# Reordering four places of a second transformer block (gates, delta-rule rounds, latent attention, merge) in a fused Trainium2 kernel

## The reference, cut to what matters

```python
# h: modulated, normalised tokens (1024 channels); ctx: the same of the context
q, k, v = split(silu(centred_conv(h @ w_qkv, width 5)))      # 8 heads of 128
q, k = l2norm(q), l2norm(k)
beta = sigmoid(h @ w_beta)                                   # 8 heads, 2 directions
g = -exp(a_log) * softplus(h @ w_decay + dt_bias)            # log decays
# gated delta rule, both directions, S is 128 x 128 for each head:
#   S_t = exp(g_t) S_{t-1} (I - beta_t k_t k_t^T) + beta_t k_t v_t^T ; o_t = S_t^T q_t / sqrt(128)
# in chunks, with (I + A)^{-1} by a triangular solve for each chunk
o_gdn = rms(o_fwd + o_bwd) * silu(h @ w_z)
# latent attention: 8 heads, low-rank queries (384) and keys/values (256), a 64-wide rotated part
q, k = rms(cq @ w_uq), rms(ckv @ w_uk (+ shared rotated part)); o_mla = softmax(q k^T / sqrt(192)) (ckv @ w_uv)
y = sigmoid(h @ w_g1) * (o_gdn @ w_b1) + sigmoid(h @ w_g2) * (o_mla @ w_b2)
x = x + gate * (y @ w_out);  x = x + gate * (square(relu(h2 @ w_1)) @ w_2)
```

## Time and profile before

| | |
|---|---|
| time, median of 3 runs | 4273.75 us (4262.18 to 4285.06) |
| the profiled execution's own time | 4275.11 us |
| its span in the profile | 4273.3 us |
| mean granted clock of PE | 0.947 of full |
| busy PE / PEld | 3979.9 us (93%) / 3206.5 us (75%) |
| busy DVE / ACT / POOL | 2269.3 (53%) / 1311.8 (31%) / 1578.0 us (37%) |
| chain that ended last, by engine | PE 76%, DVE 14%, issue 3%, POOL 3%, ACT 3%, DMA 1% |
| `decays` / `gdn` / `mla` / first of `merge` | from 2646 / 2674.3 / 3363.6 / 3675.9 us |

### The profile page before, as it was taken

One profiled execution on the slowest core, in us unless ns is written; L12 is line 12 of the kernel. 1 busy time (PEld: TensorE's weight loads), 2 busy tenths in 40 slices (PEclk: granted clock), 3 DMA queues, 4 the chain that ended last, 5 costly groups with the idle time before them and its releaser, 6 DMA issues.

```text
span 4273.3 us, 50376 instructions
## 1 busy us (share of the span) xinstructions
PE 3979.9 (93%) x20030; PEld 3206.5 (75%) x20030; DVE 2269.3 (53%) x3216; ACT 1311.8 (31%) x1774; POOL 1578.0 (37%) x862
## 2 busy tenths in 40 slices
PE   7997999989999999999979998878898899899999
PEld 6756888777888888876568887767777666787887
DVE  6598525475514451575985245556775448414322
ACT  3332222355222322233322223423332225423221
POOL 3312444311444244433124442467676000243443
PEclk9998999999999899999989998889899789999999
DMA  6211232311232223222013321111112122222232
GB/s 187 90 40 50 109 113 80 112 40 70 84 119 84 87 80 122 88 75 99 30 50 127 113 87 48 44 43 52 39 46 64 52 90 73 75 91 82 90 109 73
DMA packets 101226, 342.56 MB, mean 80 GB/s; under 512 B 44416, under 2 KB 47616, under 8 KB 72320
## 3 DMA queue, kind: packets, MB, share of 16 engines
q1 hardware_dynamic: 85520, 293.78, 19.9%
q10 hardware_dynamic: 15472, 45.56, 3.5%
HBM read 322.00 MB, written 17.30 MB: 79 GB/s over the span
## 4 chain that ended last, share of the span: by engine, by line
PE 76%; DVE 14%; issue 3%; POOL 3%; ACT 3%; DMA 1%; SPq 0%; DVEq 0%; ACTq 0%; POOLq 0%
PE bank L1049 18%; PE bank L1050 18%; PE bank L1051 18%; PE bank L1257 2%; PE bank L1552 1%; PE bank L1554 1%; PE bank L1553 1%; DVE work L3181 1%; PE bank L1282 1%; POOL tab L880 1%; PE bank L1803 1%; POOL tab L878 1%; PE bank L1247 1%; PE bank L1872 1%; PE bank L1832 1%
## 5 line engine op out<-in xcount | busy, mean ns | idle before, releaser
L898 POOL TENSOR_TENSOR w_lo<-ring,w_hi 128x2048 fp32r<-128x2048 f32 (+2 forms) x200 | 776.5, 3883 | 1130.0 <-ACT w_hi L2012 1101.3
L1049 PE MATMUL bank<-x_hi,w_hi 128*128 128x512 f32 x1584 | 617.4, 390 | 3.9 <-POOL w_lo L898 3.9
L1051 PE MATMUL bank<-x_hi,w_lo 128*128 128x512 f32 x1584 | 616.4, 389 | 0.0
L1050 PE MATMUL bank<-x_lo,w_hi 128*128 128x512 f32 x1584 | 616.2, 389 | 0.0
L2012 ACT ACTIVATE w_hi<-ring 128x2048 fp32r<-128x2048 f32 (+2 forms) x200 | 322.1, 1611 | 712.8 <-PE bank L1051 711.8
L1049 PE MATMUL bank<-h_hi,w_hi 128*128 128x512 f32 x960 | 373.9, 389 | 0.4
L1050 PE MATMUL bank<-h_lo,w_hi 128*128 128x512 f32 x960 | 373.5, 389 | 0.0
L1051 PE MATMUL bank<-h_hi,w_lo 128*128 128x512 f32 x960 | 373.5, 389 | 0.0
L1049 PEld LDWEIGHTS bank<-x_hi,w_hi 128*128 128x128 f32 x1584 | 297.4, 188 | 66.9 <-POOL w_lo L898 5.2
L1051 PEld LDWEIGHTS bank<-x_hi,w_lo 128*128 128x128 f32 x1584 | 297.3, 188 | 62.0
L1050 PEld LDWEIGHTS bank<-x_lo,w_hi 128*128 128x128 f32 x1584 | 297.4, 188 | 61.0
(11 more groups left out here) (555 smaller groups left out, 8318.9 us busy)
## 6 DMA issues: line engine op xcount, KB each, us to landing
ring<-stream SPq DMA_DIRECT2D x194, 1024.0 KB, 4.8
ring<-stream SPq DMA_DIRECT2D x64, 704.0 KB, 4.0
ring<-stream SPq DMA_DIRECT2D x36, 512.0 KB, 3.4
ring<-stream ACTq DMA_DIRECT2D x17, 1024.0 KB, 4.9
xn<-first_mods SPq DMA_DIRECT2D x8, 1024.0 KB, 6.8
x<-x_keep ACTq DMA_DIRECT2D x3, 2048.0 KB, 8.7
ring<-stream SPq DMA_DIRECT2D x4, 1088.0 KB, 5.8
bias_rows<-work ACTq DMA_DIRECT2D x1, 4096.0 KB, 45.9
```

Of the source, the lines that this page charges most:

```text
L898: nc.gpsimd.tensor_tensor(w_lo[:, j % 2, 0:cols], ring[:, places[k], 0:cols], w_hi[:, j % 2, 0:cols], ALU.subtract).then_inc(wlo_set, 1)
L1049: mm(b[:], hi[:, at + k, :], rhs_hi, start=(k == 0), stop=False)
L1050: mm(b[:], hi[:, at + k, :], rhs_lo[:, k, :], start=False, stop=False)
L1051: ins = mm(b[:], lo[:, at + k, :], rhs_hi, start=False, stop=(k == kt - 1))
```

## The change

Six things, in the order of time.

1. In `decays` DVE does the gate sums first, then four of the eight low parts of the activations (`low_rows`, L3114 before), the gates when ACT has delivered, the other four, and the context's low parts (L3117 before) last.
2. PE gets products whose result is overwritten, `warm(b, n)`: n products of 128 x 512 from `x_hi_g` into a bank that the next product starts afresh. In each round that has a recurrence there are 4 ahead of `lows(.., "low2")`, 1 ahead of `tr` and 4 ahead of `sn` at step 4, 3 ahead of `ks` at step 5, 4 ahead of `outs` at step 5, and, while there is a new head, 6 ahead of the last `products`: 8 x 16 + 6 x 6 = 164.
3. The low part of head 2's second weight block goes from POOL (behind the first solve) to DVE (end of round 1, behind `after(new, 1)`).
4. In a round's tail `low_qz(new+1, 0)` goes ahead of the convolution of v, and `low_qz(new+1, 1)` from there to behind the output's norm, right ahead of `before(new, 0)`; ACT's `high_qz(new+1)` goes ahead of `projected("v")`.
5. In `mla` the previous pair's norm sums stand between the products of `k_proj`, and q tiles 0 and 1 ahead of `norm_rows`; for the last pair, columns 0 to 9 stand ahead of `scores(0)` and 10 to 19 behind.
6. The merge's first gate product is issued in `mla` ahead of `turned(30)` (`first_gate`).

```diff
+                def warm(b, count_):
+                    for _ in range(count_):
+                        mm(b[:], x_hi_g[:, 0, 0:P], x_hi_g[:, 1, :], start=True, stop=True)
...
                 def ks(h, s):
+                    b = r_tile("ks", h, s)
+                    if s == CH - 1:
+                        warm(b, 3)
                     out_of(R_AT, ("sn", h, s - 1), r_drained)
-                    b = r_tile("ks", h, s)
...
                     if live:
                         tr(old, 5)
+                        last = r_tile("o", old, CH - 1)
+                        warm(last, 4)
                     if 0 <= out_ < GH:
                         rows("no", out_, t, 10, 4)
...
-                        for c in range(3):
+                        for c in range(2):
                             products(new, c)
+                        if live:
+                            out_of(R_AT, ("o", old, CH - 1), r_drained)
+                            warm(last, 6)
+                        products(new, 2)
...
@@ POOL, gdn
-                    if h + 2 <= GH:
+                    if 0 < h <= GH - 2:
                         low_kv(h + 2)
@@ PE, mla: k_proj
+                        pe.wait_ge(mla_sq, 9 + 7 * p)
+                        b_sums = aux_tile(("sums", p - 1))
...
                             for k in range(2):
+                                if p:
+                                    cs = parts[j][1]
+                                    norm_sums(p - 1, b_sums, [8 + CH * i + c for c in cs[len(cs) // 2 * k:len(cs) // 2 * (k + 1)]])
+                                    ins_sums = norm_sums(p - 1, b_sums, [4 * i + 2 * j + k])
                                 ins = mm(b, w[:, 9 + 2 * i + k, :], ckv[:, k, part], start=(k == 0), stop=(k == 1))
                             ins.then_inc(acc_full, 1)
...
-                    if p:
-                        sums(p - 1)
                     k_proj(p, w)
                     if p:
+                        q_proj(p, w, range(2))
                         norm_rows(p - 1)
...
-                    q_proj(p, w)
+                    q_proj(p, w, range(2 if p else 0, 3))
...
-                sums(PAIRS - 1)
+                pe.wait_ge(mla_sq, 9 + 7 * PAIRS)
+                b = aux_tile(("sums", PAIRS - 1))
+                norm_sums(PAIRS - 1, b, range(10))
                 scores(0)
+                norm_sums(PAIRS - 1, b, range(10, 20)).then_inc(aux_full, 1)
...
+                    if k == MLA_UNITS - 2:
+                        first_gate()
                     turned(k)
@@ ACT, gdn
+                        high_qz(new + 1)
                         projected("v", new, 2, SEQ)
-                        high_qz(new + 1)
@@ DVE, decays
-                for k in range(DT):
-                    dve.wait_ge(xg_hi_set, k + 1)
-                    signal(tt_(xn_r[:, k, :], xn[:, k, :], x_hi_g[:, k, :], ALU.subtract), xg_lo_set)
-                for j, (ks, v) in enumerate(hc_parts):
-                    dve.wait_ge(hc_hi_set, j + 1)
-                    signal(tt_(hc_lo[:, ks, :], hc[:, ks, :], v, ALU.subtract), hc_lo_set)
...
                 signal(stt(s_, u, -1.0, u, ALU.mult, ALU.min), gate_set)
+                low_rows(range(4))
                 dve.wait_ge(soft_set, 1)
...
+                low_rows(range(4, DT))
+                for j, (ks, v) in enumerate(hc_parts):
+                    dve.wait_ge(hc_hi_set, j + 1)
+                    signal(tt_(hc_lo[:, ks, :], hc[:, ks, :], v, ALU.subtract), hc_lo_set)
@@ DVE, gdn
+                    if new < GH:
+                        low_qz(new + 1, 0)
                     conv(new, 2, (0,))
...
                     conv(new, 2, (2,))
-                    if new < GH:
-                        low_qz(new + 1, 0)
...
-                    if new < GH:
-                        low_qz(new + 1, 1)
                     if live:
                         tr(old, 5)
...
                         signal(tt_(o_gdn[:, out_, :], o, o_gdn[:, out_, :], ALU.mult), head_set)
+                    if new < GH:
+                        low_qz(new + 1, 1)
                     before(new, 0)
                     before(new, 1)
                     after(new, 0)
                     before(new, 2)
                     after(new, 1)
+                    if new == 1:
+                        dve.wait_ge(kv_hi_set, 3)
+                        signal(tt_(ring_r[:, B_RAW, 0:2 * DT * P], ring[:, B_RAW, 0:2 * DT * P], ring_r[:, B_HIGH, 0:2 * DT * P],
+                                   ALU.subtract), kv_lo_set)
```

More of the change, by code:

```diff
@@ L1767, in gdn @@
                     if live:
-                        outs(old, 5)
+                        outs(old, CH - 1, last)
                     if new < GH:
@@ L1779, in gdn, with merge_halves, first_gate @@
                         out_of(table, name, drained_)
+            def merge_halves(j):
+                if j:
+                    blk.take()
+                    n["split"] += 1
+                    pe.wait_ge(wlo_set, n["split"])
+                return (merge_whi[j % 2][:].rearrange("p (w m) -> p w m", m=P),
+                        ring_r[:, places[starts[("merge", 0)] + j], :].rearrange("p (w m) -> p w m", m=P))
+            def first_gate():
+                blk.take()
+                n["split"] += 1
+                pe.wait_ge(wlo_set, n["split"])
+                hi, lo = merge_halves(0)
+                split_product(hi, lo, 0, x_hi_g, xn_r, DT)
             def mla(_):
@@ L1815, in rows, with norm_sums @@
                     ins.then_inc(aux_full, 1)
+                def norm_sums(p, b, columns):
+                    for at in columns:
+                        if at < 8:
+                            i, c = at // 4, at % 4
+                            ins = column(b, at, [(q_sq[:, i, chunk(c)], ones[:, 0:1]), (q_sq[:, 2, chunk(c)], half[:, i, 0:1])])
+                        else:
+                            i, c = (at - 8) // CH, (at - 8) % CH
+                            ins = column(b, at, [(k_sq[:, i, chunk(c)], ones[:, 0:1])])
+                    return ins
                 def k_proj(p, w):
@@ L1841, in v_proj @@
                         ins.then_inc(acc_full, 1)
-                def sums(p):
-                    pe.wait_ge(mla_sq, 9 + 7 * (p + 1))
-                    b = aux_tile(("sums", p))
-                    for i in range(2):
-                        for c in range(4):
-                            column(b, 4 * i + c, [(q_sq[:, i, chunk(c)], ones[:, 0:1]), (q_sq[:, 2, chunk(c)], half[:, i, 0:1])])
-                    for i in range(2):
-                        for c in range(CH):
-                            ins = column(b, 8 + CH * i + c, [(k_sq[:, i, chunk(c)], ones[:, 0:1])])
-                    ins.then_inc(aux_full, 1)
                 def norm_rows(p):
@@ L1938, in merge @@
             def merge(_):
-                def halves(j):
-                    blk.take()
-                    n["split"] += 1
-                    pe.wait_ge(wlo_set, n["split"])
-                    return (merge_whi[j % 2][:].rearrange("p (w m) -> p w m", m=P),
-                            ring_r[:, places[starts[("merge", 0)] + j], :].rearrange("p (w m) -> p w m", m=P))
                 for m in range(DT):
@@ L3106, in low_qz, with low_rows @@
                 signal(tt_(ring_r[:, A_RAW, at], ring[:, A_RAW, at], ring_r[:, A_HIGH, at], ALU.subtract), qz_lo_set)
+            def low_rows(ks):
+                for k in ks:
+                    dve.wait_ge(xg_hi_set, k + 1)
+                    signal(tt_(xn_r[:, k, :], xn[:, k, :], x_hi_g[:, k, :], ALU.subtract), xg_lo_set)
             def decays(_):
```

33 lines of the change are left out of this document (22 added, 11 removed).

## The result

The changed kernel took 4299.06 us, median of 6 runs (4292.72 to 4301.44), and the kernel before 4275.82 on the same chip: ratio 1.0054, 95% interval [1.0034, 1.0073]. It is slower by 23 us where 17 were to be gained. The profiled execution spans 4293.9 us at a granted clock of 0.948, 20.6 longer than before at 0.947.

What follows compares the result with a forecast made beforehand. PE, busy 93%, was taken as the bound, so gains come only where it waits or runs slow. Terms -4.5 - 3.9 - 0.5 + 0 + 1 - 8 - 0.5 - 1 = -17.4 gave 4256 us, range 4234 to 4279.

Steps and rivals of the forecast that it cites:

- Decays and round 0: Reordered DVE and ACT work starts the rounds earlier (-4.5 us) and shortens PE's wait in round 0's tail (-3.9).
- The 3.9 us of stop: Decays: time above 1.6 us in DVE's 5.50 us context part, held by POOL, said to go when they no longer meet.
- The low part moved to DVE: Round 2 starts 2.1 to 2.5 us sooner, against 2.0 lost in POOL's first solve; taken as -0.5 us.
- The rounds' tails: Rounds 2 to 7: gains and losses in front are lost in POOL's hold of DVE; sum 0, bounds -8 and +8 us.
- R3: Rival, chance 0.09: the z low part, now in the chain, is stopped by POOL in six rounds; +21 us, 4295.
- Its argument against: Against the slower rival: the low part comes free where POOL already stops the norm, and is past where POOL comes later.
- The bound of +8 us for the tails' sum: Upper limit on the change over the six tails of rounds 2 to 7, taken as 0.
- the range: Whole kernel: 4234 to 4279 us, from the faster rival to the one with absorbed moves; the slower rival stays outside.
- The sign that I had named for being wrong: The prediction is wrong if the rounds' sum moves by more than 8 us, or the spread sums still fall to 0.6.
- The attention: Latent attention: sums spread between wide products mostly keep the clock, less a new stall before q; -8 us, bounds -11 and -3.
- The last sums and the merge: Last pair's sums cut around `scores(0)`, -0.5 us; merge's first product moved, merge waits 5.5 longer, attention's end faster, -1.
- The forecast's total, -17: Whole kernel: all terms summed to -17.4 us, giving 4256 us.

Runs made afterwards that it cites:

- e11: Kernel before with only the decays' order of the changed kernel: 4273.52 us, ratio 0.9992.
- e12: Kernel before with the decays' order, the q low part's order and ACT's order of the changed kernel: 4259.52 us, ratio 0.9959.
- e2: Kernel before with only the z low part moved, to ahead of the first `before`: 4304.66 us, ratio 1.0070.
- e1: Changed kernel with only the z low part put back behind the reciprocals: 4257.97 us, ratio 0.9959 to the kernel before.
- e15: Kernel before with only the output norm's second operation moved behind `after(new, 1)`: 4266.16 us, ratio 0.9977.
- e10: Changed kernel, z low part and head 2's k and v low part put back, output norm's second operation behind `after(new, 1)`: 4255.22 us, ratio 0.9943.

## Why the prediction was wrong

- **Decays and round 0**: right, -4.8 and -5.6 for -4.5 and -3.9, but shared out otherwise. With the decays' order alone (e11) round 0 is already 2.9 shorter (54.4 to 51.5), which the prediction did not have; its own reordering adds -2.8 (e12, 48.7). The 3.9 us of stop was read too small: by the rows it is 5.50 less 1.22, 4.3.
- **The low part moved to DVE**: the price (2.0) was right and the gain nothing, not 2.1 to 2.5: the solved blocks came as late as before.
- **The rounds' tails**: the failed step, 0 for +23.4. I gave the z low part 1.25 us in the chain, and wrote of round 6 that it "falls in the same span at 3158 to 3159.3, ahead of POOL", and that POOL starts "at a time of its own". It does not: in the changed kernel's round 6 the copy held the norm and POOL's low part held the z low part for 5.45 us. The tail starts the solve, the solve ends in the next tail, and what I had not followed is POOL's copy ahead of its low part: it holds the norm and so sets DVE half a microsecond behind the low part's start. The kernel before's round 3 had shown it; I had taken the rounds for two kinds, norm or L3199 stopped by the low part, and missed this third. The mechanism was my rival R3 (4295, and 4299 was measured), which I gave 0.09. Its argument against, that the low part comes free where the norm was stopped, holds for a norm stopped by the low part (e2, rounds 5 and 6) and not for one stopped by the copy. The bound of +8 us for the tails' sum rested on this as well, and so did the range, which left R3 out. The sign that I had named for being wrong, rounds that move by more than 8 us, came.
- **The attention**: -8 for +1.7; by the medians above the spread alone costs about 3. The spread did what was said where it stands. Windows of the changed kernel: the three interleaved stretches, then the q tiles behind the first of them, and the first pair's untouched k and q products (to 3403.5 they take 20.5 us, and took 17.2 at 0.97 before):

```profile
3408.60:3421.80 13.20, 11.63 (x74) 9.14 (x73) 1.43 (x7) 1.84 (x5) 0.00 (x0) 0.98 0.41 159
3442.00:3455.00 13.00, 11.54 (x73) 9.07 (x71) 1.31 (x6) 1.74 (x4) 0.00 (x0) 1.00 0.42 162
3475.60:3490.80 15.20, 15.20 (x73) 12.00 (x71) 0.34 (x2) 0.38 (x1) 0.00 (x0) 0.73 0.36 139
...
3421.80:3427.00 5.20, 5.20 (x9) 2.35 (x10) 3.27 (x7) 3.55 (x8) 0.00 (x0) 0.73 0.18 25
...
3383.00:3400.00 17.00, 16.07 (x51) 9.09 (x50) 5.98 (x12) 5.21 (x10) 0.00 (x0) 0.78 0.00 0
```

  From the sums' start to the q tiles it takes 13.15, 13.15 and 16.8 us with the stall (1.57 in the first), 5.8 less than the 48.9 of the earlier trace rows. But the rest of a pair, 18.7 us each time before, takes 20.2, 20.5 and 20.7, 5.3 more, the q tiles now at a clock of 0.73; and the first pair's k and q products take 3.3 more at 0.78. The low clock came elsewhere. I had counted its going and not where it would come; why it comes there, no run shows. The step that failed here is the overlooked rest of a pair; that the spread does not pay is shown by the 18 profiles, not by this one alone.
- **The last sums and the merge**: from the last sums to the turn 22.8 us for 23.7, -0.9 for -0.5. The product moved makes the end 1.2 longer, for 5.5 us of products taken out of it, as I had argued; with the attention's end shorter by a little more, the -1 stands within what the profiles tell (-2 by medians).

The forecast's total, -17, is what e1 measured (-0.41%), and that is a coincidence: the attention gave none of its 8, and the tails, with the z low part at its old place, gave 11 where I had 0. The solves got 1.5 us longer by the decays' order (e11), 7.3 shorter by q low part and ACT's order (e12 over e11) and 5.2 shorter by the rest of e1; by what way, no run tells.

## What to carry to other kernels

Before an operation is moved on DVE, ask of it not what it costs alone but what POOL runs there: with two SBUF operands, or one at the doubled rate, it waited here for the whole of a POOL instruction that reads SBUF (over 4 us for a low part). Behind one such wait, where POOL's next instruction follows at once (here 0.08 us later), the next such operation meets it as a rule, not by chance. Put such operations where a delay is not in the chain, or cut POOL's instruction into pieces. An operation whose result is wanted late does not belong in a chain's last steps: the output norm moved back gave 10.5 us in the solves of the kernel before (e15), though only 2.1 in one where it was stopped less (e10).

## What was not expected of the hardware

A single instruction of each round, moved past ten others on one engine, made the kernel before 0.7% slower (e2), since it took 5.4 us for 1.2 in three rounds. In the changed kernel it did so in four. POOL's 4.5 us instruction itself took 4.8 to 4.9 us wherever DVE's norm ran into its start, and 5.37 where the z low part did (round 3 of the changed kernel), so both engines lose.
